# Experts of a mixture: seven raw weight slots and three for upper halves, upper halves multiplied one unit ahead, eight groups written out, last sums left in PSUM

## The reference, cut to what matters

```python
def hier_moe(h, w_group, b_group, w_expert, b_expert, w1, w3, w2):
    g_w, g_idx = lax.top_k(softmax(hf @ w_group + b_group), 1)      # one group a token
    top_v, top_i = lax.top_k(e_sel, TOP_K)                          # two experts of that group
    gate = (g_w * softmax(top_v))
    # each expert, over its own tokens:
    return (jax.nn.silu(xb @ w1[e]) * (xb @ w3[e])) @ w2[e]
x = x + hier_moe(h, ...)            # the gated sum over a token's experts
return rms_norm(x, final_norm)      # the output, 256 x 1024
```

## Time and profile before

| what | us |
|---|---|
| median of 3 runs | 1820.88 (1817.76 to 1822.51) |
| the profiled execution: its own time | 1818.44 |
| its span, first to last instruction | 1816.7 |
| PE, DVE, ACT busy in the span | 1738.0, 1578.1, 1219.9 |

### The profile page before, as it was taken

How to read it: one execution, slowest core, us unless ns; L and a number is a source line. 1 busy time by engine, 2 the same in 40 slices (tenths; PEclk the granted TensorE clock), 3 DMA queues, 4 the chain that set the end, 5 groups by cost and what they waited for, 6 DMA issues and landing times.

```text
span 1816.7 us, 25139 instructions
## 1 busy us (share of the span) xinstructions
PE 1738.0 (96%) x9700; PEld 1483.4 (82%) x9700; DVE 1578.1 (87%) x1375; ACT 1219.9 (67%) x952; POOL 126.9 (7%) x140
## 2 busy tenths in 40 slices
PE   8999999999999999999999999999999999999997
PEld 7977888899888889888877877778777787778775
DVE  6787778789677776678999999999999999999997
ACT  5465444444343355446788888889888898888985
POOL 1255000000000010440000000000000000000000
PEclk9999999999999999999999999999999999999999
DMA  7521355653345455226799999999999999999994
GB/s 287 192 93 70 139 197 184 228 224 140 139 177 201 177 206 223 94 105 267 309 428 428 428 428 426 428 429 428 429 428 429 428 428 429 428 429 428 429 428 194
DMA packets 41239, 544.16 MB, mean 300 GB/s; under 512 B 4704, under 2 KB 4832, under 8 KB 6496
## 3 DMA queue, kind: packets, MB, share of 16 engines
q1 hardware_dynamic: 41184, 543.39, 72.9%
HBM read 542.33 MB, written 1.05 MB: 299 GB/s over the span
## 4 chain that ended last, share of the span: by engine, by line
PE 61%; DMA 11%; issue 7%; ACT 6%; DVE 5%; POOL 0%; DVEq 0%; ACTq 0%; POOLq 0%; SPq 0%
PE psum L1465 17%; DMA ring<-in_w 11%; PE psum L1010 9%; PE psum L859 7%; PE psum L1027 7%; PE psum L1012 5%; PE psum L1479 4%; ACT arena_r L1879 4%; DVE ring_r L2415 3%; PE psum L1494 2%; PE psum L902 2%; PE psum L1229 1%; PE psum L919 1%; PE psum L1403 1%; PE psum L1367 1%
## 5 line engine op out<-in xcount | busy, mean ns | idle before, releaser
L2415 DVE TENSOR_TENSOR ring_r<-ring,arena_r 128x4096 fp32r<-128x4096 f32 x192 | 847.4, 4422 | 17.0 <-ACT arena_r L1879 13.5
L1879 ACT ACTIVATE arena_r<-ring 128x4096 fp32r<-128x4096 f32 x188 | 682.3, 3629 | 62.4 <-DMA ring<-in_w 60.8
L1465 PE MATMUL psum<-arena_r,stream_r 128*128 128x512 f32 x1024 | 410.6, 401 | 11.8 <-DVE stream_r L2505 9.0
L1465 PE MATMUL psum<-ring_r,stream_r 128*128 128x512 f32 x1024 | 403.2, 394 | 0.0
L1010 PE MATMUL psum<-stream_r,arena_r 128*128 128x512 f32 x704 | 250.7, 399 | 1.8 <-DVE stream_r L1966 1.7
L1465 PEld LDWEIGHTS psum<-arena_r,stream_r 128*128 128x128 f32 x1024 | 194.8, 190 | 56.7 <-DVE ring_r L2415 11.0
L1663 ACT ACTIVATE arena_r<-ring 128x3072 fp32r<-128x3072 f32 x40 | 111.0, 2775 | 180.9 <-DMA ring<-in_ffn 180.9
L1465 PEld LDWEIGHTS psum<-ring_r,stream_r 128*128 128x128 f32 x1024 | 194.8, 190 | 38.6
L1012 PE MATMUL psum<-stream_r,ring_r 128*128 128x256 f32 x704 | 197.9, 281 | 0.0
L1494 PE MATMUL psum<-arena_r 128*128 128x512 f32 x512 | 161.3, 396 | 12.1 <-DVE arena_r L2564 11.3
L859 PE MATMUL psum<-stream_r,ring_r 128*128 128x256 f32 x968 | 167.4, 285 | 0.0
(11 more groups left out here) (338 smaller groups left out, 2477.8 us busy)
## 6 DMA issues: line engine op xcount, KB each, us to landing
ring<-in_w SPq DMA_DIRECT2D x192, 2048.0 KB, 12.9
ring<-in_ffn SPq DMA_DIRECT2D x44, 1536.0 KB, 6.4
ring<-in_w_in SPq DMA_DIRECT2D x8, 2048.0 KB, 7.8
ring<-in_out_w SPq DMA_DIRECT2D x7, 2048.0 KB, 7.7
ring<-in_in_w SPq DMA_DIRECT2D x6, 2048.0 KB, 10.9
ring<-in_l_in SPq DMA_DIRECT2D x8, 1536.0 KB, 8.6
ring<-in_proj SPq DMA_DIRECT2D x2, 2048.0 KB, 7.9
ring<-in_in_w SPq DMA_DIRECT2D x2, 1024.0 KB, 9.6
```

Of the source, the lines that this page charges most:

```text
L1465: last = mm(dst, xg[:, k, :], b[:, k * D_EXPERT:(k + 1) * D_EXPERT], start=(k == 0 and b is u_hi), stop=(k == KD - 1 and b is u_lo))
L1879: A(w_hi[u % HI_SLOTS], ring[:, MOE_SLOT[at], :], ACT.Copy).then_inc(m_hi, 1)
L2415: V.tensor_tensor(ring_r[MOE_SLOT[u % NM]][:, :], raw, w_hi[u % HI_SLOTS].bitcast(F32), ALU.subtract).then_inc(m_lo, 1)
```

## The change

The raw matrices get a seventh slot (`RAW_SLOTS`), made of a former `w_hi` buffer, so three `w_hi` are left. ACT makes `hi` of unit v + 3 ahead of the results of unit v, as soon as DVE and the new upper products are done with unit v. PE multiplies the upper halves of unit v + 1 (`high_products`) before the lower halves of unit v (`low_products`), except for w2 of the last expert of a group, whose upper halves come right before its lower ones. `gather` moves two units up. The loop over groups is written out. For the last unit `lo` comes in two halves. Four matmuls put `x` itself into PSUM in the last group, `send_last` adds the experts' part on top, and ACT and DVE take squares and output from there; the output leaves in three pieces.

```diff
-HI_SLOTS = 4
+HI_SLOTS = 3
+RAW_SLOTS = SLOTS + 1
@@ SP
+            for v in range(RAW_SLOTS):
+                if MOE_BEFORE[v]:
+                    sp.wait_ge(*MOE_BEFORE[v])
+                expert_load(v)
...
+                for v in range(RAW_SLOTS, N_UNITS):
+                    sp.wait_ge(m_unit, units + (v - RAW_SLOTS + 1))
+                    expert_load(v)
@@ PE
+            def high_products(v, p, units):
+                g, (kind, e) = v // NM, MOE[v % NM]
+                pe.wait_ge(m_hi, units + (v + 1))
+                if kind == "w2":
+                    pe.wait_ge(m_hT_lo, p * N_EXPERTS + (g * PER_GROUP + e + 2))
...
+                elif e >= 1:
+                    pe.wait_ge(m_raw, p * (2 * N_EXPERTS) + (g * (2 * PER_GROUP) + 2 * e - (1 if kind == "w1" else 0)))
+                products(v, False).then_inc(m_hi_used, 1)
...
-                with pe.Fori(0, N_GROUPS) as g:
+                for g in range(N_GROUPS):
...
+                    high_products(v0, p, units)
+                    for u in range(NM):
+                        if u == NM - 1:
+                            high_products(v0 + u, p, units)
+                        elif u < NM - 2:
+                            high_products(v0 + u + 1, p, units)
+                        low_products(v0 + u, p, units)
...
+                        elif u in (8, 10, 12):
+                            pe.wait_ge(m_selT, n + 1)
+                            residual_in_bank((u - 8) // 2)
+                        elif u == NM - 4:
+                            residual_in_bank(3)
+                send_last(n)
@@ ACT
-                act.wait_ge(m_unit, n * NM + (u - HI_SLOTS + 1))
+                act.wait_ge(*moe_landed(v, p))
+                act.wait_ge(m_lo, units + (v - HI_SLOTS + 1))
+                act.wait_ge(m_hi_used, units + (v - HI_SLOTS + 1))
...
+                        if v + HI_SLOTS < N_UNITS:
+                            split_hi(v + HI_SLOTS, p, units)
+                        results(u, n)
@@ DVE
+                        if v + 2 == N_UNITS - 1:
+                            last_lo(n, units)
+                        else:
+                            if 1 <= v and v + 2 < N_UNITS:
+                                split_lo(v + 2, units)
+                            hidden(u, n)
...
-                add_back(n)
-            scaled_norm("last", out_ready, 48)
+            V.tensor_tensor(h_raw[:, 0, 0, :], psum[:, LAST_BANK[2], :], norm_row[:, 0:512], ALU.mult).then_inc(x_gained, 1)
+            for tc, h in ((0, 0), (0, 1), (1, 1)):
```

More of the change, by code:

```diff
@@ L1454, in _, with product @@
             end("rank", mm(bank("rank")[:, 16:24], ones, g_hot[:, 1, :], start=False, stop=True))
[L1455 to L1467, removed]
+            def product(v, low, i, h):
+                kind, e = MOE[v % NM]
+                w = MOE_LOW[v % RAW_SLOTS] if low else w_hi[v % HI_SLOTS]
+                if kind != "w2":
+                    return mm(psum[:, H1_BANK if kind == "w1" else H3_BANK, :], xg[:, i, :],
+                              w[:, i * D_EXPERT:(i + 1) * D_EXPERT], start=(i == 0 and not low),
+                              stop=(i == KD - 1 and low), skip_group_check=True)
+                return mm(psum[:, Y_BANK[h], :], hT[:, e % 3, i, :], w[:, i * D + h * 512:i * D + (h + 1) * 512],
+                          start=(e == 0 and i == 0 and not low), stop=(e == PER_GROUP - 1 and i == NE - 1 and low),
+                          skip_group_check=True)
@@ new lines, in low_products @@
+            def low_products(v, p, units):
+                if v < N_UNITS - 1:
+                    pe.wait_ge(m_lo, units + (v + 1))
+                    products(v, True).then_inc(m_unit, 1)
+                else:
+                    pe.wait_ge(m_lo_half, p + 1)
+                    for j in range(NE // 2):
+                        for h in range(2):
+                            product(v, True, j, h)
+                    pe.wait_ge(m_lo, units + (v + 1))
+                    for h, done in enumerate((m_y_half, m_unit)):
+                        for j in range(NE // 2, NE):
+                            last = product(v, True, j, h)
+                        last.then_inc(done, 1)
@@ new lines, in _ @@
+                        if u == GATHERED_AT and g < N_GROUPS - 1:
+                            gathered_lo(n + 1)
+                            gates_in_fold(n + 1)
+                    for i in range(2):
+                        result_lo(i, n)
+                with dve.If(p + 1 < passes):
+                    following = dve.snap(p * N_UNITS + N_UNITS)
+                    for v in range(HI_SLOTS):
+                        split_lo(v, following)
+            last = NORMS["last"]
+            dve.wait_ge(row_in, 48)
```

321 lines of the change are left out of this document (173 added, 148 removed).

## The result

| kernel | median, us | runs | ratio to before, 95% |
|---|---|---|---|
| before | 1818.08 (1816.92 to 1822.51) | 20 | |
| changed | 1824.51 (1821.76 to 1830.86) | 20 | 1.0036 (1.0028 to 1.0044) |

The change makes the kernel 0.36% slower, 6.4 us between the medians. The forecast was 1821.0 with no change as the likeliest case; the range held the time. That the time came within 3.5 us of 1821.0 is in part luck: the forecast started from 1820.88, the median of three runs, where twenty give 1818.08. The change by itself was forecast at +0.1 and measured at +6.4 (5.1 to 8.0), about the 5.5 us from which on the forecast called a kernel slower. The profiled execution of the changed kernel took 1828.51 us, 4.0 above its median, so its own sums come out larger than the change is worth: 10.0 us between the two spans, of which 2.4 lie ahead of the expert stage.

What follows compares the result with a forecast made beforehand. The DMA engines were taken to bound the kernel; -1.9 + 0 + 3.5 + 0.7 - 2.2 = +0.1 moved the profiled execution from 1818.44 to 1818.5 us, the median forecast being 1821.0, range 1814.5 to 1830.

Steps and rivals of the forecast that it cites:

- no change: Whole kernel: the time stays within about 0.3%, 5.5 us, of before; chance 0.60, with its own range from 1816 to 1826.
- Start of the stream: Start of the expert stage's loads: a seventh load ahead against later slot releases, -1.9 us in sum (-3.1 to -1.0).
- One load fewer: Before the expert stage: the seventh slot lets one more load go out in an idle stretch, -4.9 us.
- The first release: Start of the stage: the first slot is freed behind 24 matmuls, 8 more at 0.23 us each, +1.8 us.
- The next releases: After the first release: five in PE's new order take 25.7 us, over 5 x 4.9, +1.1 us (0 if loads cover it).
- The middle: Middle of the expert stage: the DMA stream keeps the pace and hides the new order, 0 us.
- The 6.5 us to spare: Middle, seven slots: a unit's slot is freed some 18.5 us after landing, leaving 6.5 before its next load is late.
- One sign of being wrong: Expert stage: the prediction would be wrong if ACT waits for PE ahead of `hi` in every group.
- Written-out groups: Seven more groups fetch their own code, 28 more q8 packets, delaying full DMA engines: +3.5 us (1.1 to 31).
- Last landing to last product: End of the stage: PE's backlog makes it finish 14.1 us after the last landing against 13.3, +0.7 us taken.
- From there to the end: From PE's last product to the kernel's end: the new sums, squares and output pieces give -2.2 us (-1.2 to -3).
- The rival on fetches: Expert stage: PE's fetches go round four engines, +8 to +11 us in place of 3.5, about 1827; chance 0.17.

Runs made afterwards that it cites:

- PE in turn: Changed kernel with each unit's upper products right before its own lower ones, never one unit ahead; ratio to before 1.0000 (0.9991 to 1.0009).
- the clean case: Changed kernel with PE one unit ahead in groups two to seven only, not in the first and last; ratio to before 0.9996 (0.9987 to 1.0005).

## Why the prediction was off, by its steps

- **Start of the stream.** One load fewer: -4.9, measured -5.2 (with PE in turn). The first release: +1.8, measured +1.7. The next releases: +1.1, measured +3.6. The walk had the wait for `h_raw` of unit 0 (0.6), but not the table load that the new order puts behind a wait, nor the half clock after PE's wait; the run with the table load moved gave 3.2 of it back. The start is worth nothing then (-4.9 + 1.7 + 3.6 = +0.4), not -1.9.
- **The middle.** 0, and it held: one unit ahead in the middle groups costs nothing that could be told. The 6.5 us to spare were too many. One slot less should have left 6.5 - 4.9 = 1.6, and it broke the stream for 21 us. One sign of being wrong came in seven groups: ACT waits 1.1 us for PE ahead of one `hi` in each. No unit landed late there.
- **Written-out groups.** The mechanism held (a packet sets one full engine back, nothing is caught up), but the size was off. +3.5 was between sixteen engines in turn (2.2) and dealing by chance (5); measured were 6.3 for all engines' code, 6.7 in the changed kernel. In the clean case a loss of 1.5 comes with each eighth packet, so (28 + 4)/8 = 4 hits of 1.5 = 6 was the sum to make; its trace has five hits, 7.8, against the 1.6 that the kernel before loses at units 9, 14 and 19, so +6.2. The duration of a packet (1.1) was also taken for what it costs (1.5), and 13 small packets of ACT, DVE and SP, which I had counted as a third hit at most, can cost 3.5 alone.
- **The page's rule.** The Trainium skill (Runtime: NRT & Kernel Launch, section Instruction fetch mechanics) has the refills' cost mostly hidden and says that kernels prefer to be unrolled. By that this term would be 0. The runs don't agree: 0.39% for the written-out groups, with DMA engines that are full.
- **Last landing to last product.** +0.7, measured +2.4. From PE's restart to its end 28.8 - 4.2 = 24.6 were forecast, and 24.8 came (1791.74 to 1816.5), with 0.9 for the matmul of `x`. It began 1.4 late, with the granted clock at 0.66 just ahead: two half units there took 3.32 and 2.42, and 2.11 and 1.98 in the run with the table load moved, 1.6 less. Where no such dip stood there (the run with the table load moved), PE ended 13.9 behind the landing, 0.2 from the forecast 14.1. That is one execution each.
- **From there to the end.** -2.2, measured -1.9; the last issue came 6.9 behind PE's end as forecast, the end 0.3 later.
- **Sum.** +0.1 forecast, 6.4 between the medians: 2.5 from the slow releases, about 3 from the fetches, 0.5 to 1.7 from PE's backlog, 0.3 from the end. The rival on fetches (four engines in turn, 9 to 12) had the period wrong, but stood nearer than the forecast.
- **Slips.** The five releases are 1.2 over, not 1.1; the start adds up to -2.0, not -1.9; the last issue at +7.0 and 3.05 after it are +10.05, not +9.9; the slices are at nine tenths from the twenty-first on. None of them changes the forecast by more than 0.3.

Open: why PE begins the stage 2.4 later in the changed kernel's profiled execution (in eight other versions of it the first matmul of the stage stands between 870.9 and 873.1, so this is no fixed price of the change); what lowers the granted clock after one wait and not after another of the same length; and what decides which DMA engine a fetch lands on.

## What to carry to other kernels

When all DMA engines are full, count instruction fetches as delays that stay: a hardware loop over groups is worth 0.39% here (0.25 to 0.52), and it pays to write out only the parts that must differ (first and last group). The reordering was free in the middle groups and was paid for at both ends; there it could be left out. Look at what an engine does first behind a moved wait: a one-time cost such as a table load that lay in idle time may then lie in the chain.

## What the runs showed of the hardware

- Each eight 16 KB packets of PE's instruction queue, about 1.1 us each on one DMA engine, made a stream of full engines 1.5 us later for good. In one kernel each eighth packet took all of it, in the changed kernel three in a row shared it.
- Thirteen more 8 KB packets of the other engines' queue, 0.3 us each on a DMA engine, cost 3.5 us in one kernel. The costs of the two queues didn't add: 3.5 and 8.5 alone, 6.3 together.
- The granted clock fell to half (0.57 in 4 us) right behind a wait of PE of 1.57 us, and eight matmuls took 3.69 us in place of 2.11. With a wait of 0.34 at that place it stayed full, but it also did behind waits of 1.58 us (985.69) and 3.02 us (1193.38) elsewhere in the same trace.
- ACT's table load (1.28 us) was issued ahead of the wait of the `h_raw` that needed it in the kernel before and with ACT's results first (870.16 and 870.47), and behind the wait where a `hi` needed it first (876.04). That `hi` waits for two semaphores at once and the `h_raw` for one; whether this decides it was not tested.
